# Attention block: values' product with the queries on partitions, division behind it, output transposed back, and a new closing of the output projection's first units

## The reference

```python
q = (h @ w_q + b_q) * 64 ** -0.5            # 16 heads of 64, 4 key/value heads
# per head and block of 128 queries: 256 keys (the block before and its own)
s = where(band, q @ k.T - slope * dist, -inf)
m = max(max(s), sink)
p = exp(s - m)
denom = sum(p) + exp(sink - m)
o = (p @ v) / denom
h = h + o @ w_o + b_o
```

## Time and profile before

| | |
|---|---|
| median of 3 runs | 1992.65 us (1991.84 to 1993.42) |
| the profiled execution | 1992.73 us, span from first to last instruction 1990.9 us |
| PE / PE weight loads busy | 1914.8 us (96%) / 1552.7 us (78%) |
| DVE / ACT / POOL busy | 1236.1 us (62%) / 756.8 us (38%) / 287.9 us (14%) |
| mean granted TensorE clock | 0.988 of full speed |

### The profile page before, as it was taken

How to read it: one execution, slowest core, us unless ns; L and a number is a source line. 1 busy time by engine, 2 the same in 40 slices (tenths; PEclk the granted TensorE clock), 3 DMA queues, 4 the chain that set the end, 5 groups by cost and what they waited for, 6 DMA issues and landing times.

```text
span 1990.9 us, 29477 instructions
## 1 busy us (share of the span) xinstructions
PE 1914.8 (96%) x10634; PEld 1552.7 (78%) x10634; DVE 1236.1 (62%) x1850; ACT 756.8 (38%) x1366; POOL 287.9 (14%) x215
## 2 busy tenths in 40 slices
PE   7999899999998899999999999999999999999997
PEld 6888678888887677777778788888777787888886
DVE  6996454333334777777755755747678657567474
ACT  4234344233233434443424432424446534334242
POOL 2532232111022100000011100101200011001012
PEclk9999999999998999999999999999999999999999
DMA  5222323232322111111113232222321122322222
GB/s 189 95 97 95 112 68 106 95 103 87 105 91 79 47 51 59 59 49 49 54 38 106 74 112 89 95 95 95 114 77 43 54 85 91 110 85 95 95 95 85
DMA packets 46945, 170.47 MB, mean 86 GB/s; under 512 B 5344, under 2 KB 5504, under 8 KB 46720
## 3 DMA queue, kind: packets, MB, share of 16 engines
q1 hardware_dynamic: 45648, 165.12, 25.1%
q10 hardware_dynamic: 1200, 3.95, 0.6%
HBM read 166.94 MB, written 2.11 MB: 85 GB/s over the span
## 4 chain that ended last, share of the span: by engine, by line
PE 74%; DVE 7%; ACT 3%; issue 2%; POOL 0%; DVEq 0%; POOLq 0%; ACTq 0%
PE ps L246 16%; PE ps L248 16%; PE ps L247 16%; PE ps L258 6%; PE ps L260 5%; PE ps L259 5%; PE ps L668 1%; PE ps L644 1%; PE ps L559 1%; DVE scr L1146 1%; DVE w_lo L226 1%; ACT scr L1318 1%; ACT Y L1318 1%; DVE scr L848 1%; PE ps L297 1%
## 5 line engine op out<-in xcount | busy, mean ns | idle before, releaser
L226 DVE TENSOR_TENSOR w_lo<-w_raw,w_hi 128x1024 fp32r<-128x1024 f32 x293 | 395.2, 1351 | 178.6 <-ACT w_hi L221 178.4
L221 ACT ACTIVATE w_hi<-w_raw 128x1024 fp32r<-128x1024 f32 x304 | 317.1, 1049 | 242.2 <-PE ps L248 169.4
L246 PE MATMUL ps<-A_hi,w_hi 128*128 128x512 f32 x950 | 369.8, 389 | 2.1 <-issue 2.0
L248 PE MATMUL ps<-A_hi,w_lo 128*128 128x512 f32 x950 | 369.6, 389 | 0.0
L247 PE MATMUL ps<-A_lo,w_hi 128*128 128x512 f32 x950 | 369.6, 389 | 0.0
L246 PE MATMUL ps<-B_hi,w_hi 128*128 128x512 f32 x724 | 283.4, 391 | 3.2 <-issue 2.4
L247 PE MATMUL ps<-B_lo,w_hi 128*128 128x512 f32 x724 | 282.4, 390 | 0.0
L248 PE MATMUL ps<-B_hi,w_lo 128*128 128x512 f32 x724 | 282.4, 390 | 0.0
L246 PEld LDWEIGHTS ps<-A_hi,w_hi 128*128 128x128 f32 x950 | 178.3, 188 | 40.0 <-issue 3.1
L248 PEld LDWEIGHTS ps<-A_hi,w_lo 128*128 128x128 f32 x950 | 178.3, 188 | 37.2
L247 PEld LDWEIGHTS ps<-A_lo,w_hi 128*128 128x128 f32 x950 | 178.4, 188 | 36.8
(11 more groups left out here) (285 smaller groups left out, 2595.4 us busy)
## 6 DMA issues: line engine op xcount, KB each, us to landing
w_raw<-d_ws SPq DMA_DIRECT2D x304, 512.0 KB, 3.5
X<-d_xT SPq DMA_DIRECT2D x4, 512.0 KB, 7.1
X<-d_xT ACTq DMA_DIRECT2D x1, 2048.0 KB, 8.6
d_out<-X SPq DMA_DIRECT2D x4, 512.0 KB, 2.6
scr<-gc_rows ACTq DMA_DIRECT2D x7, 256.0 KB, 3.1
cst<-d_cst SPq DMA_DIRECT2D x1, 800.0 KB, 11.8
par<-d_par SPq DMA_DIRECT2D x1, 344.5 KB, 3.1
scr<-d_pw SPq DMA_DIRECT2D x1, 256.0 KB, 11.9
```

The costliest lines, as they stand in the source:

```text
L221: nc.scalar.activation(w_hi[:, c], raw[:, c], ACT.Copy).then_inc(S(f"w_hi{s}"), 1)
L226: nc.vector.tensor_tensor(w_lo[:, c], raw[:, c], w_hi[:, c].bitcast(F32), ALU.subtract)\
L246: pe.matmul(ps[bank][:], w_hi[:, c], hi, start=k == 0, stop=False)
L248: last = pe.matmul(ps[bank][:], w_lo[:, c], hi, start=False, stop=k == n - 1)
```

## The change

The probabilities are transposed as they come from the exponential. In `values_pe` the transposed probabilities (128 keys by 128 queries) are the stationary operand and 64 columns of values the moving one, so the queries come out on partitions and the divisor is one number per partition and head. DVE divides the whole output tile at once (`outputs`), PE transposes it back in the same PSUM bank (`outputs_pe`, four transposes), and ACT copies it as before. The sum and reciprocal of both heads are taken together (`denominators`). The output projection is closed as that of the delta rule layer, with its first four units in four banks.

```diff
         def transpose_pe(pe, t, e):
-            pe.wait_ge(S("s_n"), count("s_n", 8 * t + 4 * e + 4))
+            pe.wait_ge(S("s_e"), count("s_e", 5 * (2 * t + e) + 5))
...
         def values_pe(pe, t):
...
                 for b in (2 * n, 2 * n + 1):
-                    for half_ in range(0 if b else 1, 2):
-                        col = b * 256 + half_ * P
-                        for e in range(2):
+                    for e in range(2):
+                        for half_ in range(0 if b else 1, 2):
+                            col = b * 256 + half_ * P
                             key = (b - 1 + half_) * P + 64 * e
-                            last = pe.matmul(ps[6 + t % 2][64 * e:64 * e + 64, b * P:(b + 1) * P],
-                                             VA_T[t % 2][:, key:key + 64], PT[t % 2][e][:, col:col + P],
+                            last = pe.matmul(ps[6 + t % 2][:, b * P + 64 * e:b * P + 64 * e + 64],
+                                             PT[t % 2][e][:, col:col + P], VA_T[t % 2][:, key:key + 64],
                                              start=half_ == 0 or b == 0, stop=half_ == 1)
+        def outputs_pe(pe, t):
+            pe.wait_ge(S("s_ot"), count("s_ot", t + 1))
+            for b in range(NCH):
+                last = pe.transpose(chunk(ps[6 + t % 2], b), chunk(OT, b), ident)
+            last.then_inc(S("s_of"), 1)
...
                 part(t + 2, cuts[0], cuts[1])
+                if t:
+                    outputs_pe(pe, t - 1)
                 if t < KT - 1:
                     scores_pe(pe, t + 1, 1)
...
-            residual_pe(pe, U_BO, pairA, wait_o, late=2, begun=True)
+            def whole(s, first, end):
+                open_segment(pe, rnd(U_BO, 0), s, pairA, first, end, wait_o, 4)
+            whole(2, 0, KT - 2)
+            outputs_pe(pe, KT - 1)
+            for s in range(3):
+                whole(s, KT - 2, KT - 1)
+            whole(3, 0, KT - 1)
+            for s in range(SLOTS):
+                whole(s, KT - 1, KT)
+            for s in range(SLOTS):
+                (unit_after_opening if s < 2 else unit)(pe, rnd(U_BO, 1), s, pairA)
...
+            def output_hi(t):
+                act.wait_ge(S("s_of"), count("s_of", t + 1))
+                a.activation(tile(pairA[0], t), ps[6 + t % 2][:], ACT.Copy).then_inc(S("t_hi"), 1)
             for t in range(KT):
-                if t < KT - 2:
-                    ahead(act, split_hi, rnd(U_Q, (t + 2) // SLOTS), (t + 2) % SLOTS)
+                ahead(act, split_hi, rnd(U_Q, (t + 2) // SLOTS), (t + 2) % SLOTS)
+                if t:
+                    output_hi(t - 1)
                 by_keys(t, 0)
                 if t < KT - 1:
                     exps(t + 1, 0)
                 by_keys(t, 1)
                 if t < KT - 1:
                     exps(t + 1, 1)
-                act.wait_ge(S("s_o"), count("s_o", t + 1))
-                a.activation(tile(pairA[0], t), ps[6 + t % 2][:], ACT.Copy).then_inc(S("t_hi"), 1)
-            residual_act(act, U_BO, "n_f1", "f_norm1", pairB)
+            output_hi(KT - 1)
+            residual_act(act, U_BO, "n_f1", "f_norm1", pairB, opened=True)
...
-            def normalise(t, e):
...
+            def denominators(t):
+                dve.wait_ge(S("s_e"), count("s_e", 10 * t + 10))
+                v.tensor_tensor(mx_heads(t, M_DEN), mx_heads(t, M_SUM), mx_heads(t, M_SINK), ALU.add)\
                     .then_inc(S("s_n"), 1)
+                dve.wait_ge(S("s_n"), count("s_n", 2 * t + 1))
+                v.reciprocal(mx_heads(t, M_INV), mx_heads(t, M_DEN)).then_inc(S("s_n"), 1)
+            def outputs(t):
+                dve.wait_ge(S("s_o"), count("s_o", t + 1))
+                dve.wait_ge(S("s_n"), count("s_n", 2 * t + 2))
+                if t:
+                    dve.wait_ge(S("s_of"), count("s_of", t))
+                inv = mx_heads(t, M_INV).rearrange("p e b -> p b e").unsqueeze(3).broadcast_to([P, NCH, 2, 64])
+                v.tensor_tensor(o_heads(OT), o_heads(ps[6 + t % 2][:]), inv, ALU.mult).then_inc(S("s_ot"), 1)
...
-            normalise(0, 0)
-            normalise(0, 1)
             for t in range(KT):
                 more = t < KT - 1
+                if t:
+                    outputs(t - 1)
                 if more:
                     scored(t + 1, 0)
-                if t < KT - 2:
-                    ahead(dve, split_lo, rnd(U_Q, (t + 2) // SLOTS), (t + 2) % SLOTS)
+                ahead(dve, split_lo, rnd(U_Q, (t + 2) // SLOTS), (t + 2) % SLOTS)
+                if more:
+                    scored(t + 1, 1)
                 if t:
                     output_lo(t - 1)
                 if more:
-                    scored(t + 1, 1)
                     maxima(t + 1, 0)
                     maxima(t + 1, 1)
-                    normalise(t + 1, 0)
-                    if t + 2 < KT:
-                        q_tile(t + 2)
-                    normalise(t + 1, 1)
+                denominators(t)
+                if t + 2 < KT:
+                    q_tile(t + 2)
+            outputs(KT - 1)
             output_lo(KT - 1)
-            residual_dve(dve, U_BO, "n_f1", "f_norm1", pairB, bias="b_o")
+            residual_dve(dve, U_BO, "n_f1", "f_norm1", pairB, bias="b_o", opened=True)
```

More of the change, by code:

```diff
@@ L1185, in build @@
         DD = carve(T)
+        OT = carve(T)
         def sc3(t, e):
@@ L1194, in build, with mx_heads, o_heads @@
         M_SUM, M_SINK, M_NEG, M_MAX, M_DEN, M_INV = range(6)
+        def mx_heads(t, n):
+            return MX[:, 48 * (t % 2):48 * (t % 2 + 1)].rearrange("p (e n b) -> p e n b", e=2, n=6)[:, :, n, :]
+        def o_heads(ap):
+            return ap.rearrange("p (b e d) -> p b e d", b=NCH, e=2)
         def half_rows(ap, e):
@@ L1400, in maxima @@
                     .then_inc(S("s_mx"), 1)
-            def normalise(t, e):
[L1404 to L1410, removed]
-                sc = SC[t % 2][e][:, P:2 * P]
-                v.tensor_scalar(sc, sc, inv[:, 0:1], None, ALU.mult).then_inc(S("s_n"), 1)
-                v.tensor_tensor(sc3(t, e)[:, 1:NCH], sc3(t, e)[:, 1:NCH],
-                                inv[:, 1:NCH].unsqueeze(2).broadcast_to([P, NCH - 1, 256]), ALU.mult)\
-                    .then_inc(S("s_n"), 1)
+            def denominators(t):
+                dve.wait_ge(S("s_e"), count("s_e", 10 * t + 10))
+                v.tensor_tensor(mx_heads(t, M_DEN), mx_heads(t, M_SUM), mx_heads(t, M_SINK), ALU.add)\
+                    .then_inc(S("s_n"), 1)
+                dve.wait_ge(S("s_n"), count("s_n", 2 * t + 1))
[7 more added lines that the diff above has]
+                v.tensor_tensor(o_heads(OT), o_heads(ps[6 + t % 2][:]), inv, ALU.mult).then_inc(S("s_ot"), 1)
             def output_lo(t):
```

## The result

The changed kernel takes 2003.89 us, the median of five runs (2002.17 to 2008.61), against 1992.65 us (1989.90 to 1993.62) for the kernel before on the same chip. The ratio is 1.0064 with an interval of 1.0052 to 1.0077: slower by 10.4 to 15.3 us. The forecast of 2001.8 us had the sign and the mechanism; the time is 2.1 us above it by the median and 3.6 by the ratio, which puts it at 2005.4, just outside the stated range of 1995.5 to 2005. The profiled execution, the one read here, took 2003.89 us.

A forecast was written before the change was run, and what follows sets the result against it. DVE was taken to set the loop's 12.19 us round, PE 1.15 us behind being full. Later sixth-iteration scores 3.6, end 4.0 and clock 1.5 sum to 9.1 us on 1992.7: 2001.8 us, range 1995.5 to 2005.

The forecast's parts named there:

- the term for the clock at the loop's start: Around PE's wait before the first product: a clock fall was thought likelier than none; 1.5 us, between 0 and 2.7.
- The product's pace: In values_pe: 0.107 us a record, 3.1 us a product; 1.4 us more a tile, 11.4 us over eight tiles.
- The transposes back: On PE between the projection part and scores_pe(t+1, 1): four take 0.43 us a tile, 3.4 us in all, without waiting.
- The ring and the iteration: In the loop: scores, scored, output_lo, maxima, exps, by_keys take 7.30 us up to the product; a round 13.28 against 12.19.
- The beginning: Before the loop: DVE reaches scored(1, 0) earlier, PE waits 3.15 us, first product at 1488.9; 1.9 us gained.
- The end: From the sixth iteration's scores_pe(7, 1) to the fifth output unit: 34.6 us against 30.6, with a 0.45 us wait.
- The third rival: In the loop: half clock for the whole stretch and once more, from waits before each product; 2005.7 us, 7%.
- a product near 1.68 us: Rival in values_pe: halved moving columns, hidden weight load, so the product keeps its 1.68 us; 1990.4 us, 11%.
- 0.081 us a record: Rival in values_pe: pace half way between the trace's two forms, 5.5 us less than the forecast; 1996.3 us, 8%.
- DVE was freed: DVE's round falls to 9.2 us; the rival, DVE still held by output_lo, split_lo and outputs, had 2%, some 2004 us.

The follow-up runs named there:

- the two runs on the widths: The changed kernel's values' product with 64 instead of 128 weight columns (narrow): 1990.68 us; or with 128 instead of 64 moving columns (wide): 1999.99 us.
- the run with the seventh wait filled: The changed kernel with six projection matmuls of the output projection's second unit moved in front of the seventh values' product: 2003.03 us, ratio 1.0061.
- the old closing: The changed kernel with the output projection closed as before (two units closed, then two more): 2007.28 us, ratio 1.0075.
- early scores: The changed kernel with split_lo put behind scored(1, 1) and maxima(1, 0) in the first round alone: 2003.98 us, ratio 1.0063.
- both edits: The changed kernel with output_lo(t-1) behind maxima(t+1, 0), and split_lo behind scored(1, 1) and maxima(1, 0) in the first round: 1996.21 us, ratio 1.0019.
- the run with GpSimd alone: The kernel before with only the low parts of the loop's six weight units moved from DVE to GpSimd: 1990.44 us, ratio 0.9987.

## Where the prediction held, and the step that failed

The step that failed is the term for the clock at the loop's start: 1.5 us in the sum, 3.1 measured. The other steps of the stage held to within 0.6 us. The profiled executions give 2.2 of the 3.6 us by the ratio. The rest is put down to falls of the clock outside the stage, which the prediction took for fixed; two profiles show such falls, but not their mean over all runs.

Taken on the profiled execution, whose loop began 0.29 us late (1478.07 here against 1477.78), the fifth unit comes 11.3 us later than in the kernel before, whose own stands here, where 9.1 were forecast:

```profile
1588.34 0.39 PE L246 MATMUL ps<-A_hi,w_hi 128*128 128x512 f32 x1
```

Step by step:

- **The product's pace**: right. 3.24 to 3.27 us, forecast 3.1, inside 1.68 + 1.2 to 1.6; the two runs on the widths show that the weight load is what sets it. The estimate of 0.107 lay between the forms of the earlier trace rows; the upper of them, 0.112, was it.
- **The transposes back**: right, 0.60 us by the record, 0.11 each in the iteration, as the run with one of them shows.
- **The ring and the iteration**: right. 13.40 us on average from 1498.44 to 1565.44 against 13.28, 0.6 us over five iterations. The ring is 1559.32 - 1552.02 = 7.30 us, as forecast; the other part, 1552.02 - 1545.90 = 6.12, is 0.14 above the sum of 3.1, 2.45 and 0.43, which is the product, 3.24.
- **The beginning**: the first product was forecast at 1488.9 and stands at 1489.14 - 0.29 = 1488.85; the wait was 3.03 against 3.15.
- **The end**: 1599.94 - 1565.44 = 34.50 us against 34.6, the fifth unit's wait 0.48 against 0.45.
- **The clock at the start**: this is the step that failed, in its size. `scores_pe(2, 1)` was to start at 1494.9 with the clock held, and starts at 1498.44 - 0.29 = 1498.15; 0.17 of that is the product, 3.1 us are the half clock, where the prediction said "part of the slow stretch would lie in the wait" and took 1.5 us out of 0 to 2.7. The windows show the opposite: the wait passed at 1.00 and the whole stretch of 6.8 us fell on a PE with work queued. The upper bound, 2.7 us, was low as well: the same work as from 1484.01 to 1490.13 takes 3.3 us by the earlier trace rows, not 3.4, so the fall cost 2.8 us in the kernel before. There, too, nearly all of the stretch lay on work. The clock fell some 0.4 us before the wait's end:

```profile
1483.00:1484.00 1.00, 0.00 (x0) 0.00 (x0) 1.00 (x3) 0.00 (x0) 0.00 (x0) 0.79 0.00 0
```

The sum is 9.1 + 0.17 + 1.6 + 0.6 - 0.1 = 11.4 us; measured are 11.3.

That stands against a span that grew by 11.2 us, since the profiled execution of before had the 1.6 us fall in the feed-forward layer and that of after had not, but 1.1 us more at the end: 0.29 + 11.3 - 1.6 + 1.1 = 11.1. The ratio over all runs, in which such falls are spread over both kernels, says 12.8 us. The prediction took the profiled execution of before for its base and so took its falls for fixed, which they are not; it had nothing to tell that from, with one profile.

The third rival, the half clock "for the whole stretch and once more", had 7% and 2005.7 us. Half of it is in the profiled execution (the whole stretch, 3.1 us), and the run with one transpose shows the "once more" at 3.2 us. That its 2005.7 is so near to the 2005.4 of the ratio is luck, since no profile of the changed kernel itself has the second fall. Its reason was another than the rival's: not the wait of 0.3 us in each iteration, behind which the clock stayed at full in every profile, but the single wait of 1.70 us before the seventh product. What carries single runs of the changed kernel on to 2008 is the clock, by their mean granted clock, but where it falls in them stays open. From the lowest, 2002.2, the seventh product (3.2), the feed-forward layer (1.6) and the end (1.1) add up to 2008.1, but the run with the seventh wait filled reached 2008.84 as well, and no profile fell on such a run.

The other rivals fell: a product near 1.68 us is what 64 weight columns give (1.77), and nothing with 128 ran at 0.081 us a record; DVE was freed, as its waits in every iteration show.

## What to carry to other kernels

Turning a round of small float32 matmuls like these is priced by the columns of the weights, not by the moving ones: count records times weight columns on either side before asking what it saves elsewhere. Where another engine is the bound by a tenth, first look for work of its own to move (here to GpSimd) and for the order at the loop's edges; that gave 7 us where the change cost 13. In these runs a wait of PE of 1 us or more costs its own length and, as a chance, up to 3.2 us of half clock on what stands behind it, so such a fall is priced in full and not shared with the wait; matmuls that are due later can fill it. A single profile doesn't tell which falls belong to the kernel: compare stretches, and several executions.

## What the runs showed of the hardware that was not expected

- Moving columns cost nothing between 64 and 128 beside weights of 128: 3.27 and 3.32 us for 28 float32 records.
- The granted clock did not fall in the changed kernel's first wait but behind it, with PE at work again: 1.00 over the wait, 0.50 from about 1490.7, 1.5 us into the product. In the loop it stayed down for 6.8 us or for 3.4, and the price followed: 3.1 to 3.2 us or about 1.6. Removing the first fall was followed by one at the seventh product, behind an unchanged wait.
- The same wait goes both ways. The seventh product's 1.70 to 1.72 us left the clock up in five profiles (the changed kernel twice, the narrow and the wide product, the old closing) and brought it down in two (early scores, one transpose); 1.03 us before the first product brought it down once (both edits) and left it up at 1.01 to 1.02 us in three others. Behind the first product's 3.0 us it fell in all eight profiles that have that wait. What decides behind the shorter ones was not found.
- GpSimd took 2.37 us for a low part that takes DVE 1.22, and DVE's instructions kept their times beside it. But the first low part took 3.03 us: it began while DVE was multiplying two operands that both lie in SBUF (L1416), the later ones beside rows that read PSUM. In the run with GpSimd alone the first one, which overlaps less of such a row, took 2.78 us. DVE's 0.95 us were the same each time. The Trainium skill's "GPSIMD Engine Reference", section "Key points", says that the two contend where DVE has two SBUF inputs, and these two rows agree; no run was made to test it.
